# First attention's output product by pairs of feature tiles, most of it behind the units of the attention

## The chip, the cores and the metric

The kernel runs on one core of one Trainium2 chip. The metric is the device time of one execution in microseconds (us). TensorE (PE) multiplies, VectorE (DVE), ScalarE (ACT) and GpSimd (POOL) work on elements, SyncE (SP) issues the loads. Each engine takes its own instructions in their order; a wait at the head of an engine's queue holds all that stands behind it.

## What is computed

Two transformer-like blocks run after one another on 512 tokens of width 1024; the change lies in the second block's first attention, a windowed attention with 16 query heads of 64 features and 2 key heads, over the 512 tokens and 256 context tokens:

```python
def softmax_with_sink(s, sink):
    m = jnp.maximum(jnp.max(s, axis=-1, keepdims=True), sink)
    p = jnp.exp(s - m)
    return p / (jnp.sum(p, axis=-1, keepdims=True) + jnp.exp(sink - m))
...
def window_gqa(hx, hc, wq, wk, wv, wo, sink, cos, sin, need_ctx):
...
    out_x = jnp.moveaxis(ob, 0, 1).reshape(B, L, A_HEADS_2 * HEAD_DIM) @ wo
    out_c = None
    if need_ctx:
        qc = (hc @ wq).reshape(B, C, A_KV_HEADS, G, HEAD_DIM)
        s = jnp.einsum('bqhgd,bkhd->bhgqk', qc, kc).astype(jnp.float32) * scale
        p = softmax_with_sink(s, sink_f).astype(vc.dtype)
        out_c = jnp.einsum('bhgqk,bkhd->bqhgd', p, vc).reshape(B, C, A_HEADS_2 * HEAD_DIM) @ wo
    return out_x, out_c
...
        x = layer_norm(alpha * x + g1 * ax, ln1_g[i], ln1_b[i])
```

## The kernel before

All activations are kept with features on the partitions: `X` and `O` are 8 feature tiles of 128 features by 768 columns (512 tokens, then 256 context tokens; `X_CTX` names these two column ranges). Products in float32 are made from rounded halves: a weight `w` is split into `whi` and `wlo`, an activation into `Ahi` and `Alo`, and each product is three matmuls (`whi*Ahi`, `whi*Alo`, `wlo*Ahi`). Weights arrive in blocks of 128x2048 in a ring of three slots (`RING`); POOL splits each half block with two instructions (L460, L462).

The first attention is 96 **units** (`UNITS`): 4 groups of heads, in each 6 query tiles (first the two of the context, then the four of the tokens), in each 4 heads. A unit's scores have 256 keys (context), 512 or 640 keys (tokens), and one column more for the sink. So one group is 24 units: 8 of 257 columns, 4 of 513, 8 of 641, 4 of 513. The loops of all engines go by a **step** u:

- PE (L994): `window_scores` of unit u (L937 the sink, L943, L944 and L946 the keys, L953 the masks); then `window_turn` of unit u-3, which transposes its probabilities (L969, 2, 4 or 5 transposes); then in three steps of four a part of `window_values` for the four heads of an earlier tile (L983).
- DVE (L1893): the maximum of unit u (L1899); in 8 later steps and before the first ones `take_query`, the low half of a query (L1869); the reciprocal of unit u-1 (L1908); in every fourth step `take_values`, which moves values to `O` (L1853).
- ACT (L1399): `take_turned` of unit u-3, which copies the transposed probabilities to `ptA` (L1142), then the exponential of unit u (L1409), then in the steps of `TAKE_AT` (33, 35, 37, 39 and 63, 65, 67, 69 among others) the high half of a query (L1142).
- POOL (L556): scales the probabilities of unit u (L559) after its reciprocal.

The scores of unit u wait for the exponential of unit u-2, since two score buffers alternate. The turned probabilities have two PSUM buffers (banks 4 and 5 by turns; a fifth tile is put in bank 7), the values take bank 6.

After the last unit ACT and DVE split `O` tile by tile into `Ahi` and `Alo`, and `dense("woA", ...)` (L1008) multiplies it by the output weights, 8 output tiles by 8 input tiles, in all eight banks. DVE adds each output tile times `mod(0, 2, j, c)` to `X` (L1921), and the layer normalization `l1` begins with sums over all of `X` (L622). POOL splits block `B_WOA` ahead of the units, and the other blocks of this product after the last unit.

## Time and profile before

| what | us |
|---|---|
| median of 3 runs | 2848.58 |
| lowest, highest | 2844.63, 2852.0 |
| the profiled execution, its time | 2846.66 |
| its span | 2844.8 |
| PE busy in the span | 2670.7 (94%) |
| DVE, ACT, POOL busy | 1270.2, 663.3, 1332.8 |

Times in the trace are us from the span's start. A row of a timeline gives the start, the duration, the engine, the line and the tiles; x5 means five instructions merged. The busy time of a matmul includes its way through the array, so the distance from one start to the next is the better measure of its cost.

### The profile page before, as it was taken

Reading aid. Unit: us, or ns where it says so; the run is one execution under the profiler, and the core shown is the slowest. Engines: PE = TensorE matmul, PEld = TensorE weight load, DVE = VectorE, ACT = ScalarE, POOL = GpSimd, SP = SyncE. Lnnn points to the kernel's source line nnn. Section 1 sums busy time; section 2 is a strip of 40 time slices with the busy share of each in tenths; the row PEclk is TensorE's granted clock in tenths of the full one; section 3 lists DMA queues with packets and bytes.
Section 4 is the critical chain, followed back from the end, with each engine's and each line's share of the span. In section 5 each row is a group of like instructions: output and inputs, shape, how many; then the busy total and the mean of one; then the engine's idle time right before and its main releaser. Section 6 shows DMA issues by size and latency. Waiting matters only on the chain.

```text
span 2844.8 us, 39295 instructions
## 1 busy us (share of the span) xinstructions
PE 2670.7 (94%) x14668; PEld 2155.6 (76%) x14668; DVE 1270.2 (45%) x1904; ACT 663.3 (23%) x1255; POOL 1332.8 (47%) x862
## 2 busy tenths in 40 slices
PE   8989999999999989899989999999879998899997
PEld 6667777777777768666768888888668876778886
DVE  6941222252222245444354444444666554455545
ACT  2221000031000023566121110110345553211112
POOL 6356555535555553133546333444253221676661
PEclk9999999999999989899989999999999998999998
DMA  5124444434444431000111111111101100222221
GB/s 189 45 82 150 146 147 145 143 105 143 146 139 141 141 125 67 23 1 1 45 38 60 60 63 62 59 59 59 45 30 44 44 29 23 79 91 96 96 96 52
DMA packets 67369, 235.57 MB, mean 83 GB/s; under 512 B 8144, under 2 KB 9552, under 8 KB 67152
## 3 DMA queue, kind: packets, MB, share of 16 engines
q1 hardware_dynamic: 65792, 233.64, 25.0%
q8 instruction: 62, 1.02, 0.1%
q10 hardware_dynamic: 1488, 0.69, 0.1%
q14 instruction: 27, 0.22, 0.0%
HBM read 232.21 MB, written 2.10 MB: 82 GB/s over the span
## 4 chain that ended last, share of the span: by engine, by line
PE 86%; DVE 5%; issue 4%; ACT 2%; POOL 1%; DMA 1%; DVEq 0%; SPq 0%; ACTq 0%; POOLq 0%
PE ps L589 67%; PE ps L1084 2%; PE ps L780 2%; PE ps L744 2%; PE ps L983 2%; PE ps L1056 1%; PE ps L969 1%; PE ps L1106 1%; DMA raw<-in_stream 1%; DVE X L1953 1%; PE ps L708 1%; PE ps L632 1%; PE ps L937 1%; PE ps L944 1%; PE ps L789 1%
## 5 line engine op out<-in xcount | busy, mean ns | idle before, releaser
L460 POOL TENSOR_SCALAR whi<-raw 128x1024 fp32r<-128x1024 f32 x332 | 362.8, 1093 | 1189.3 <-DMA raw<-in_stream 1189.1
L462 POOL TENSOR_TENSOR wlo<-raw,whi 128x1024 fp32r<-128x1024 f32 x332 | 812.9, 2449 | 27.7
L589 PE MATMUL ps<-Ahi,whi 128*128 128x512 f32 (+1 forms) x2128 | 730.0, 374 | 37.1 <-DVE Alo L1573 17.8
L589 PE MATMUL ps<-Alo,whi 128*128 128x512 f32 (+1 forms) x2128 | 721.4, 370 | 0.0
L589 PE MATMUL ps<-Ahi,wlo 128*128 128x512 f32 (+1 forms) x2128 | 719.2, 369 | 0.0
L589 PEld LDWEIGHTS ps<-Ahi,whi 128*128 128x128 f32 x2128 | 375.9, 190 | 128.4 <-issue 21.9
L589 PEld LDWEIGHTS ps<-Ahi,wlo 128*128 128x128 f32 x2128 | 375.6, 190 | 69.5
L589 PEld LDWEIGHTS ps<-Alo,whi 128*128 128x128 f32 x2128 | 376.9, 191 | 66.9 <-issue 0.7
L589 PE MATMUL ps<-hhi,whi 128*128 128x512 f32 x1120 | 375.5, 372 | 19.5 <-DVE X L1953 18.8
L589 PE MATMUL ps<-hhi,wlo 128*128 128x512 f32 x1120 | 372.8, 370 | 0.0
L589 PE MATMUL ps<-hlo,whi 128*128 128x512 f32 x1120 | 370.2, 367 | 0.0
L1953 DVE SCALAR_TENSOR_TENSOR X<-ps,modT,X 128x512 f32<-128x512 f32 (+1 forms) x384 | 237.1, 654 | 91.5 <-PE ps L589 90.1
L1142 ACT ACTIVATE arena<-ps 128x256 f32<-128x256 f32 (+5 forms) x228 | 115.3, 519 | 629.7 <-PE ps L780 471.3
L1939 DVE TENSOR_TENSOR tmp<-tmp 128x768 f32<-128x768 f32 (+1 forms) x64 | 83.2, 1302 | 387.2 <-ACT tmp L1435 369.9
L1716 DVE TENSOR_TENSOR tmp<-ps,tmp 128x512 f32<-128x512 f32 x44 | 28.7, 687 | 490.8 <-PE ps L589 490.8
L589 PEld LDWEIGHTS ps<-hhi,whi 128*128 128x128 f32 x1120 | 192.5, 188 | 64.3 <-DVE X L1953 25.0
L589 PEld LDWEIGHTS ps<-hhi,wlo 128*128 128x128 f32 x1120 | 192.4, 188 | 39.3
L589 PEld LDWEIGHTS ps<-hlo,whi 128*128 128x128 f32 x1120 | 192.4, 188 | 38.1
L1435 ACT ACTIVATE tmp<-ps 128x512 f32<-128x512 f32 x96 | 47.1, 526 | 675.9 <-PE ps L589 673.7
L1729 DVE TENSOR_TENSOR X<-ps,X 128x512 f32<-128x512 f32 x176 | 121.4, 690 | 103.3 <-PE ps L589 100.9
L1142 ACT ACTIVATE hhi<-tmp 128x512 fp32r<-128x512 f32 (+1 forms) x108 | 74.8, 698 | 285.8 <-DVE tmp L1716 201.1
L559 POOL TENSOR_SCALAR tmp<-tmp,sm 128x256 f32<-128x256 f32 (+2 forms) x96 | 63.0, 658 | 158.8 <-DVE sm L1908 158.6
(267 smaller groups left out, 2842.2 us busy)
## 6 DMA issues: line engine op xcount, KB each, us to landing
raw<-in_stream SPq DMA_DIRECT2D x428, 512.0 KB, 3.7
X<-in_xT SPq DMA_DIRECT2D x2, 1024.0 KB, 6.5
arena<-in_dft SPq DMA_DIRECT2D x1, 2048.0 KB, 16.6
out_xT<-X SPq DMA_DIRECT2D x2, 1024.0 KB, 4.3
X<-in_ctxT SPq DMA_DIRECT2D x1, 1024.0 KB, 19.0
w<-in_stream SPq DMA_DIRECT2D x2, 512.0 KB, 4.3
vec<-in_vec SPq DMA_DIRECT2D x1, 364.5 KB, 7.6
arena<-in_fmap SPq DMA_DIRECT2D x1, 256.0 KB, 12.1
```

What stands on the lines that cost most here:

```text
L460: pool.tensor_scalar(whi[:, s, part], raw[:, s, part], 1.0, 1.0, ALU.mult, ALU.mult).then_inc(sem("w_hi"), 1)
L462: pool.tensor_tensor(wlo[:, s, part], raw[:, s, part], whi[:, s, part], ALU.subtract).then_inc(sem("w_split"), 1)
L559: pool.tensor_scalar(prob, prob, sm[:, u % 8, 2:3], 1.0, ALU.mult, ALU.mult).then_inc(sem("pA"), 1)
L589: mm = pe.matmul(dst[c], w[:, b % RING, off:off + P], rhs(k, part, c0, n), start=(k == 0 and w is whi and part == 0), stop=(k == kn - 1 an ...
L744: mm = pe.matmul(ps[:, WOUT_BANK[j], :], w[:, at:at + P], a[:, k, 0:T], start=(k == 0 and w is hi and a is Ahi), stop=(k == KT - 1 and w i ...
L780: mm = pe.matmul(ps[ADA_GROUP * g:ADA_GROUP * (g + 1), 6 + e, 0:256], csil[:, k, :], raw[:, at % RING, k * 256:(k + 1) * 256], start=(half ...
L983: mm = pe.matmul(ps[DH * h:DH * h + DH, 6, 0:2 * P], vA[:, ks[t], DH * g:DH * g + DH], heads[:, h], start=(t == 0), stop=(t == len(ks) - 1 ...
L1084: mm = pe.matmul(ps[:, 6 + t % 2, 0:256], a[:, k, t * P:(t + 1) * P], w[:, (B_QKV + 2) % RING, k * 256:(k + 1) * 256], start=(k == 0 and a ...
L1142: return act.activation(dst, src, ACT.Copy, scale=scale)
L1729: dve.tensor_tensor(X[:, m, 0:T], ps[:, 4 + m % 2, :], X[:, m, 0:T], ALU.add).then_inc(sem(f"{name}_dfree"), 1)
L1939: dve.tensor_tensor(tmp[:, j, 0:width], r, r, ALU.mult).then_inc(sem(f"{name}_mul"), 1)
L1953: mm = dve.scalar_tensor_tensor(out=X[:, m, c0:c0 + n], in0=ps[:, 4 + len(cols) * (m % (4 // len(cols))) + c, 0:n], scalar=mod(l, 5, m, c) ...
```

## The change

The product of the first attention is no longer made by output tiles over all of `O`. It is made by pairs of input tiles: pair p holds the feature tiles 2p and 2p+1 of `O`, which are complete once the 24 units of one group of heads are done. For each pair, each output tile m and each of the two column ranges c there is one **piece**: 6 matmuls of 512 or of 256 columns, and one DVE instruction that adds the result to `X`. There are 64 pieces. Of the 48 pieces of pairs 0 to 2, 46 stand at the end of PE's steps 33, 35, 36, 38, 39, ... 101 (`FILLED`), two in every three steps, even pieces 512 wide and odd ones 256 wide; they all use bank 7. The last two and the 16 of pair 3 follow after the loop, those of pair 3 in all banks. A piece waits until DVE has added the piece before it.

DVE adds the piece of PE's step u in its own step u+1, behind the maximum, `take_query`, the reciprocal and `take_values`. ACT and DVE split a pair's two tiles inside the loop (`pair_hi` in steps 32, 56, 80; `pair_lo` in steps 33, 57, 81); the weights of pairs 1 to 3 are split by POOL between the units (`pair_weights`, three smaller instructions a half block), and SP loads them with other rows and columns per block. The turned probabilities have one buffer (bank 4, a fifth tile in bank 5), and the transposes wait until the previous unit's are copied. `modulations(1)`, small DVE work, is moved ahead to the projection of the queries.

```diff
--- before.py
+++ after.py
+PIECES = [(p, m, c) for p in range(4) for m in range(KT) for c in range(2)]
+FILL_FIRST = 33
+FILLED = {FILL_FIRST + 3 * (i // 2) + 2 * (i % 2): i for i in range(48)}
+PAIR_HI = {24 * p + 32: p for p in range(3)}
+PAIR_LO = {24 * p + 33: p for p in range(3)}
+PAIR_SPLITS = {1: (4, 6, 8, 10, 12, 14), 2: (18, 20, 22, 24, 26, 28), 3: (66, 68, 70, 72, 74, 76)}
 V_FIRST = 2
...
+        def pair_split(p, kk):
+            return (Alo[:, 6 + kk, :], kd_r[:, kk, :]) if p % 2 else (Alo[:, 2 + kk, :], Alo[:, 4 + kk, :])
+        def piece_bank(i):
+            p, m, c = PIECES[i]
+            return 7 if p < 3 else 2 * (m % 4) + c
+        def piece_done(i):
+            p, m, c = PIECES[i]
+            if m % 4 == 3 and c:
+                return when("w_used", 2 * (B_WOA + p) + m // 4 + 1)
+            return when("woA_done", i + 1 - i // 8)
         def v(name, i, n=1):
             a = _cols[name][0] + i
...
             split_swiglu(1)
-            split_run(B_KV, ring_end(B_WOA))
+            split_run(B_KV, B_WOA + 1)
+            def pair_weights(p, step):
+                b, half, step = B_WOA + p, step // 3, step % 3
+                if step == 0:
+                    part = slice(half * HALF, (half + 1) * HALF)
+                    pool.wait_ge(*when(f"raw{b % RING}{half}", 16 * (b // RING) + 16))
+                    pool.tensor_scalar(whi[:, b % RING, part], raw[:, b % RING, part], 1.0, 1.0, ALU.mult,
+                                       ALU.mult).then_inc(sem("w_hi"), 1)
+                    return
+                part = slice(half * HALF + (step - 1) * 512, half * HALF + step * 512)
+                pool.wait_ge(*when("w_hi", SPLITS[b] + half + 1))
+                mm = pool.tensor_tensor(wlo[:, b % RING, part], raw[:, b % RING, part], whi[:, b % RING, part], ALU.subtract)
+                if step == 2:
+                    mm.then_inc(sem("w_split"), 1)
             for u in range(N_UNITS):
+                for p, units in PAIR_SPLITS.items():
+                    if u in units:
+                        pair_weights(p, units.index(u))
                 pool.wait_ge(*when("denA", u + 1))
                 prob = probA[u % 4][:, 1:1 + len(keys(UNITS[u][2])) * P]
...
                                        ALU.add).then_inc(sem(f"{name}_res"), 1)
-            split_run(ring_end(B_WOA), ring_end(B_ML0 + 2))
+            split_run(B_ML0, ring_end(B_ML0 + 2))
             norm_residual("l1", 1, X_CTX)
             split_run(ring_end(B_ML0 + 2), ring_end(B_QKV + 2))
...
             def turned(u, t):
-                at = (4 + u % 2) * 512 + t * P if t < 4 else 7 * 512
+                at = 4 * 512 + t * P if t < 4 else 5 * 512
                 return psf[:, at:at + P]
             def window_turn(u):
                 ks = keys(UNITS[u][2])
                 pe.wait_ge(*when("pA", u + 1))
-                pe.wait_ge(*when("ptA", u + 1))
+                pe.wait_ge(*when("ptA", u + 2))
                 for t in range(len(ks)):
-                    if t == 4:
-                        pe.wait_ge(*when("ptA", u + 2))
                     mm = pe.transpose(turned(u, t), probA[u % 4][:, 1 + t * P:1 + (t + 1) * P], ident[:, :])
                 mm.then_inc(sem("turnA"), 1)
...
+            def out_piece(i):
+                p, m, c = PIECES[i]
+                b, (c0, n) = B_WOA + p, X_CTX[c]
+                if m % 4 == 0 and c == 0:
+                    pe.wait_ge(*when("w_split", SPLITS[b] + m // 4 + 1))
+                if m == 0 and c == 0:
+                    pe.wait_ge(*when("OA_split", 2 * p + 2))
+                before = i if p < 3 or i < 56 else i - 7
+                if i > 0:
+                    pe.wait_ge(*when("woA_evac", min(before, 48) if p == 3 and i < 56 else before))
+                for kk in range(2):
+                    hi, lo = pair_split(p, kk)
+                    at = m // 2 * 512 + kk * 256 + m % 2 * P
+                    for w, o in ((whi, hi), (whi, lo), (wlo, hi)):
+                        mm = pe.matmul(ps[:, piece_bank(i), 0:n], w[:, b % RING, at:at + P], o[:, c0:c0 + n],
+                                       start=(kk == 0 and w is whi and o is hi), stop=(kk == 1 and w is wlo))
+                mm.then_inc(sem("w_used" if m % 4 == 3 and c else "woA_done"), 1)
             pe.wait_ge(*when("maskb", 2))
                 four, part = divmod(u - LEAD - 4, 4)
                 if four >= 0 and part < 3:
                     window_values(four, part)
-            dense("woA", B_WOA, X_CTX, "OA_split")
-            pe.wait_ge(*when("woA_evac", 5))
-            layernorm("l1", X_CTX, "woA_evac", 0)
+                if u in FILLED:
+                    out_piece(FILLED[u])
+            for i in range(max(FILLED[u] for u in FILLED if u < N_UNITS + LEAD + 3) + 1, len(PIECES)):
+                out_piece(i)
+            pe.wait_ge(*when("woA_evac", 48 + 10))
+            layernorm("l1", X_CTX, "woA_evac", 48, 2)
...
-                four = (4 + u % 2) * 512
+                four = 4 * 512
                 act.wait_ge(*when("turnA", u + 5))
                 act.wait_ge(*when("oA_done", u // 4 + 1))
                 if nk > 4:
-                    copy(ptA[u // 4 % 2][:, 4, h * P:(h + 1) * P], psf[:, 7 * 512:7 * 512 + P])
+                    copy(ptA[u // 4 % 2][:, 4, h * P:(h + 1) * P], psf[:, 5 * 512:5 * 512 + P])
                     nk = 4
                 copy(ptA[u // 4 % 2][:, 0:nk, h * P:(h + 1) * P],
                      psf[:, four:four + nk * P].rearrange("p (t q) -> p t q", t=nk)).then_inc(sem("ptA"), 1)
+            def pair_hi(p):
+                act.wait_ge(*when("oA", 6 * p + 7))
+                if p >= 2:
+                    act.wait_ge(*block_used(B_WOA + p - 2))
+                for kk in range(2):
+                    copy(pair_split(p, kk)[0], O[:, 2 * p + kk, :]).then_inc(sem("OA_hi"), 1)
             for u in range(N_UNITS + LEAD):
                 if u >= LEAD:
                         take_query(*TAKE_AT[u])
                     if u == KEYS_AT:
                         take_keys(1)
-            for k in range(KT):
-                if k == 0:
-                    act.wait_ge(*when("oA", 25))
-                copy(Ahi[:, k, :], O[:, k, :]).then_inc(sem("OA_hi"), 1)
+                if u in PAIR_HI:
+                    pair_hi(PAIR_HI[u])
+            pair_hi(3)
             layernorm("l1", X_CTX, 1)
...
                     take_keys(0)
                     for h in range(2):
                         take_query(0, 0, h)
+                if j == 4:
+                    modulations(1)
             for h in (2, 3):
                 take_query(0, 0, h)
             dve.wait_ge(*when("vA", 1))
                 dve.wait_ge(*when("oA_done", four + 3))
                 move(O[:, 4 * g + 2 * e:4 * g + 2 * e + 2, n * P:(n + 1) * P],
                      ps[:, 6, 0:2 * P].rearrange("p (a q) -> p a q", a=2)).then_inc(sem("oA"), 1)
+            def pair_lo(p):
+                for kk in range(2):
+                    dve.wait_ge(*when("OA_hi", 2 * p + kk + 1))
+                    hi, lo = pair_split(p, kk)
+                    dve.tensor_tensor(lo, O[:, 2 * p + kk, :], hi, ALU.subtract).then_inc(sem("OA_split"), 1)
+            def add_piece(i):
+                p, m, c = PIECES[i]
+                c0, n = X_CTX[c]
+                if i == 0:
+                    dve.wait_ge(*when("n5_res", KT))
+                dve.wait_ge(*piece_done(i))
+                dve.scalar_tensor_tensor(out=X[:, m, c0:c0 + n], in0=ps[:, piece_bank(i), 0:n], scalar=mod(0, 2, m, c),
+                                         in1=X[:, m, c0:c0 + n], op0=ALU.mult, op1=ALU.add).then_inc(sem("woA_evac"), 1)
             for u in range(N_UNITS + LEAD + 4):
                 if u < N_UNITS:
                 four, part = divmod(u - LEAD - 7, 4)
                 if four >= 0 and part == 0:
                     take_values(four)
-            for k in range(KT):
-                split_lo("OA_split", "OA_hi", k, O[:, k, :], TT)
-            dve.wait_ge(*when("n5_res", KT))
-            for j in range(8):
-                if j % 2:
-                    dve.wait_ge(*block_used(B_WOA + j // 2))
-                else:
-                    dve.wait_ge(*when("woA_done", j // 2 + 1))
-                for c, (c0, n) in enumerate(X_CTX):
-                    mm = dve.scalar_tensor_tensor(out=X[:, j, c0:c0 + n], in0=ps[:, 2 * (j % 4) + c, 0:n],
-                                                  scalar=mod(0, 2, j, c), in1=X[:, j, c0:c0 + n], op0=ALU.mult, op1=ALU.add)
-                mm.then_inc(sem("woA_evac"), 1)
-                if j == 3:
-                    modulations(1)
+                if u in PAIR_LO:
+                    pair_lo(PAIR_LO[u])
+                if u - 1 in FILLED and u - 1 < N_UNITS + LEAD + 3:
+                    add_piece(FILLED[u - 1])
+            pair_lo(3)
+            for i in range(FILLED[max(u for u in FILLED if u < N_UNITS + LEAD + 3)] + 1, len(PIECES)):
+                add_piece(i)
             layernorm("l1", X_CTX, 1)
```

In step 36 PE has, before (line numbers of before), the scores of unit 36, the transposes of unit 33, and then the next scores; `waits` lists the semaphores:

```order
L937 MATMUL ps<-vec,ident 128x1 [waits sA_free]
L944 MATMUL ps<-std_r,Ahi 128x256
L946 MATMUL ps<-std_r,Ahi 128x384
L953 MATMUL ps<-maskb 128x128 x2
L944 MATMUL ps<-rstd_r,Ahi 128x256
L946 MATMUL ps<-rstd_r,Ahi 128x384
L969 MATMUL ps<-ident,tmp 128x128 [waits ptA,pA]
L969 MATMUL ps<-ident,tmp 128x128 x3
L937 MATMUL ps<-vec,ident 128x1 [waits sA_free]
```

The same step of PE in the changed kernel, from the last matmul of the piece of step 35 (L1066 is a piece, L1000 the sink, L1030 a transpose):

```order
L1066 MATMUL ps<-Alo,wlo 128x256
L1000 MATMUL ps<-vec,ident 128x1 [waits sA_free]
L1007 MATMUL ps<-std_r,Ahi 128x256
L1009 MATMUL ps<-std_r,Ahi 128x384
L1016 MATMUL ps<-maskb 128x128 x2
L1007 MATMUL ps<-rstd_r,Ahi 128x256
L1009 MATMUL ps<-rstd_r,Ahi 128x384
L1030 MATMUL ps<-ident,tmp 128x128 [waits ptA,pA]
L1030 MATMUL ps<-ident,tmp 128x128 x3
L1066 MATMUL ps<-Alo,whi 128x512 [waits woA_evac]
```

A piece stands in front of the scores and one behind the transposes, and the second waits for DVE. On DVE the steps 33 to 35 were:

```order
L1899 TENSOR_REDUCE sm<-ps 128x1 [waits sA]
L1869 TENSOR_TENSOR q_63<-arena,q_63 64x768 [waits qs_hi]
L1908 RECIPROCAL sm<-sm 128x1 [waits sA_free]
L1899 TENSOR_REDUCE sm<-ps 128x1 [waits sA]
L1908 RECIPROCAL sm<-sm 128x1 [waits sA_free]
L1853 TENSOR_SCALAR arena<-ps 128x2x128 [waits oA_done]
L1899 TENSOR_REDUCE sm<-ps 128x1 [waits sA]
```

In the changed kernel, up to the add of the piece of step 35 in step 36:

```order
L2005 TENSOR_REDUCE sm<-ps 128x1 [waits sA]
L1958 TENSOR_TENSOR q_64<-arena,q_64 64x768 [waits qs_hi]
L2014 RECIPROCAL sm<-sm 128x1 [waits sA_free]
L1988 TENSOR_TENSOR Alo<-arena,Alo 128x768 [waits OA_hi] x2
L2005 TENSOR_REDUCE sm<-ps 128x1 [waits sA]
L2014 RECIPROCAL sm<-sm 128x1 [waits sA_free]
L1942 TENSOR_SCALAR arena<-ps 128x2x128 [waits oA_done]
L1996 SCALAR_TENSOR_TENSOR X<-ps,modT,X 128x512 [waits woA_done,res]
L2005 TENSOR_REDUCE sm<-ps 128x1 [waits sA]
L1958 TENSOR_TENSOR q_64<-arena,q_64 64x768 [waits qs_hi]
L2014 RECIPROCAL sm<-sm 128x1 [waits sA_free]
L2005 TENSOR_REDUCE sm<-ps 128x1 [waits sA]
```

The pair's low halves stand behind a `take_query`, and each add behind the maximum and the reciprocal of its step.

## Rows read from the trace of the kernel before

**Rows 1.** Window, steps 33 on: PE, PEld, DVE, ACT, POOL busy, clock, DMA, GB/s.

```profile
1232.00:1360.20 128.20, 119.17 (x869) 84.39 (x867) 59.44 (x152) 86.49 (x223) 47.97 (x68) 1.00 0.00 1
```

**Rows 2.** Timeline of the last values (PE), and the chain of waits behind it.

```profile
1358.19 1.95 PE L983 MATMUL ps<-ptA,arena 128*64 128x256 f32 x16 [0.69 <-ACT ptA L1142]
```
```profile
1363.24 69.57 PE ps L589 x384
```

**Rows 3.** Timeline, PE: one step of 641 columns with values.

```profile
1252.60 0.38 PE L937 MATMUL ps<-vec,ident 128*128 128x1 f32 x2
1253.70 0.71 PE L969 MATMUL ps<-ident,tmp 128*128 128x128 f32 x5
1254.34 1.08 PE L983 MATMUL ps<-ptA,arena 128*64 128x256 f32 x8
```

**Rows 4.** Timelines, PE: ten matmuls of 512 columns, and six of 256, apart.

```profile
2600.01 0.40 PE L589 MATMUL ps<-hhi,wlo 128*128 128x512 f32 x1
...
2602.35 0.39 PE L589 MATMUL ps<-hhi,whi 128*128 128x512 f32 x1
```
```profile
2090.41 0.28 PE L1084 MATMUL ps<-wlo,Ahi 128*128 128x256 f32 x1
...
2091.12 0.28 PE L1084 MATMUL ps<-wlo,Ahi 128*128 128x256 f32 x1
```

**Rows 5.** Waits of PE between 1232 and 1361: us, times, longest.

```profile
PE ps L969 <- POOL tmp L559: 6.7, 5, 1.7
```

**Rows 6.** Groups by form, DVE: busy and mean ns, then idle time before them.

```profile
L1899 DVE TENSOR_REDUCE sm<-ps 128x1 f32<-128x641 f32 x24 | 19.7, 820 | 14.6 <-PE ps L946 14.6
L1853 DVE TENSOR_SCALAR arena<-ps 128x256 f32<-128x256 f32 x17 | 6.9, 406 | 2.3 <-PE ps L983 2.3
L1899 DVE TENSOR_REDUCE sm<-ps 128x1 f32<-128x257 f32 x16 | 6.8, 425 | 14.7 <-PE ps L944 14.6
```
```profile
L1921 DVE SCALAR_TENSOR_TENSOR X<-ps,modT,X 128x512 f32<-128x512 f32 x8 | 6.0, 746 | 45.5 <-PE ps L589 45.5
L1921 DVE SCALAR_TENSOR_TENSOR X<-ps,modT,X 128x256 f32<-128x256 f32 x8 | 3.8, 474 | 0.0
```

**Rows 7.** Timeline of step 63, with a query taken: PE, ACT, DVE.

```profile
1288.07 0.71 PE L969 MATMUL ps<-ident,tmp 128*128 128x128 f32 x5
...
1289.47 0.80 ACT L1409 ACTIVATE tmp<-ps,sm 128x641 f32<-128x641 f32 x1
...
1291.11 0.95 DVE L1869 TENSOR_TENSOR Ahi<-arena,Ahi 64x768 fp32r<-64x768 f32 x1 [2.01 <-ACT Ahi L1142]
...
1292.17 0.81 DVE L1899 TENSOR_REDUCE sm<-ps 128x1 f32<-128x641 f32 x1
...
1292.89 0.15 DVE L1908 RECIPROCAL sm<-sm 128x1 f32<-128x1 f32 x1
```

**Rows 8.** Timeline of steps 32 and 33: transposes, maximum, next ACT copy.

```profile
1229.45 0.38 PE L969 MATMUL ps<-ident,tmp 128*128 128x128 f32 x2
...
1229.65 0.69 DVE L1899 TENSOR_REDUCE sm<-ps 128x1 f32<-128x513 f32 x1 [1.75 <-PE ps L943]
...
1230.48 0.38 PE L969 MATMUL ps<-ident,tmp 128*128 128x128 f32 x2
...
1231.06 0.37 ACT L1142 ACTIVATE ptA<-ps 128x256 f32<-128x256 f32 x1
```

**Rows 9.** Timeline after the last unit: splits of `O` beside POOL's splits of weights.

```profile
1360.64 4.51 ACT L1142 ACTIVATE Ahi<-arena 128x768 fp32r<-128x768 f32 x6 [2.51 <-DVE arena L1853]
1361.52 6.45 DVE L1542 TENSOR_TENSOR Alo<-arena,Ahi 128x768 fp32r<-128x768 f32 x3 [0.91 <-ACT Ahi L1142]
```

**Rows 10.** Page, costliest groups: POOL's low half of a weight block.

```profile
L462 POOL TENSOR_TENSOR wlo<-raw,whi 128x1024 fp32r<-128x1024 f32 x332 | 812.9, 2449 | 27.7
```

**Rows 11.** Windows of PE alone: length, busy, granted clock, DMA.

```profile
1203.00:1206.00 3.00, 3.00 (x13) 0.50 0.02 5
...
1363.30:1366.60 3.30, 3.30 (x11) 0.51 0.00 0
```

29 lines of the change are left out of this document (23 added, 6 removed).

## The prediction, made before the changed kernel was run

> **What bounds the kernel now.** I read the page first (PE busy 94%, and the chain that ended last is 86% PE), then the windows around the first attention, then PE's timeline step by step, since PE's order is what the change rewrites. Two stretches matter: the units from step 33 on, and the output product behind them. In the units PE is busy for 119.17 of 128.20 us [rows 1], so 9.0 us are idle as the profile counts it; 6.7 us of them are five waits for POOL's scaled probabilities [rows 5], which come late in the steps where a query is taken. Some more is hidden in matmul durations that include the way through the array: 0.1 to 0.2 us in about thirty steps. I take 14.5 us as the most that other work could fill there. Behind the units, the values end at 1358.19 + 1.95 = 1360.14, the product starts at 1363.24 and takes 69.57 us without a break [rows 2], up to 1432.81: 72.7 us from the last value to the end of the product. So TensorE sets the pace in both stretches. Moving multiplications from the second into the first gives nothing by itself; it can give the 14.5 us of idle time, and it costs whatever new waits PE meets.
>
> **The pieces themselves: no work saved.** 512-column matmuls follow at (2602.35 - 2600.01)/10 = 0.234 us, 256-column ones at (2091.12 - 2090.41)/6 = 0.118 us [rows 4]. A piece of six costs 1.40 or 0.71 us, a pair of pieces 2.11 us, and the 32 such pairs 67.6 us; the old product, 192 times one of each, took 69.57. Of the pieces 23 even and 22 odd ones (47.9 us) come before the last values, the rest after.
>
> **The end of the attention.** Let t be the end of the last values, on the old clock 1360.14. Piece 45 runs to t+0.7, its add to t+1.2. Piece 46 (waiting for that add) runs to t+2.7. The halves of the last two tiles of `O`: ACT starts at t+0.5 [rows 9], a copy takes 0.83, DVE's low half 0.95 if undisturbed [rows 7], but 6.45/3 = 2.15 while POOL splits weights beside it [rows 9], which it will do here as before, with blocks of the next layer. The first low half ended at about 1363.2 before, so both are done at about t+4.0. Then come the add of piece 46 (0.75), piece 47, its add, and piece 48 at t+6.0; sixteen pieces more take 16.9 us: t+22.9. Together 47.9 + 22.9 = 70.8 against 72.7: **-1.9 us**. Half a lost stretch of clock (below) is as likely here as before, so I take **-1**; from -3 to +2.
>
> **New wait 1: one bank, and the add behind the next maximum.** Even pieces from step 36 on follow an odd piece of the step before. The even piece waits for the odd one's add, which DVE has behind the maximum of this step. Count from the first transpose of the step. The maximum starts 0.20 us later [rows 8], occupies DVE for 0.72 (from 1292.17 to 1292.89 [rows 7]), the reciprocal about 0.07, the add 0.474 [rows 6], a semaphore 0.06: 1.53 us, and 1.86 in steps with `take_values` (0.406 [rows 6], 0.33 of it not overlapped). For units of 257 columns the maximum is 0.40 shorter [rows 6]. PE meanwhile has the transposes (0.64 for five up to the values, 0.54 up to a piece, 0.43 for four, 0.21 for two) and in some steps 1.0 us of values [rows 3]. With values of that length the add is hidden. Without: step 42 1.3, 54 1.3, 60 1.1, 78 1.3, 84 1.1, 90 1.3, and 45 and 93 0.2 each: **7.8 us**. Odd pieces have a whole step for the add before them and wait only where a query is taken.
>
> **New wait 2: adds behind a taken query.** In steps 33, 35, 37, 39 and 63, 65, 67, 69 DVE's `take_query` stands between the maximum and the rest, and waits for exponential and copy on ACT. In step 63 it ran from 1291.11 to 1292.06, that is 3.99 us after the transposes at 1288.07 [rows 7]. Then reciprocal and add follow: 4.0 + 0.1 + 0.47 + 0.06 = 4.6 us (4.9 with a 512-wide add of 0.746). In steps 39 and 63 PE has 1.65 us to do: 2.95 us of waiting each. In step 69 it has 1.2: 3.2. The piece of step 38 waits for an add of step 37: 4.9 less the 2.1 us of steps 37 and 38 up to the piece, 2.8; that of step 68 for one of 67, where values cover most, 0.5. In steps 36 and 66 the maximum itself starts late, behind the query of the step before: 1.3 and 2.2. Together **15.9 us**. None of these adds exists before, so the price is built from DVE's own order; its lower bound is 5 us, if ACT reaches the copies sooner because PE is slower, the upper 18.
>
> **New wait 3: the first piece of a pair.** Its operands are split inside the loop. For pairs 1 and 2: in step 56 ACT is free for `pair_hi` 1.6 us after the transposes (1229.45 to 1231.06 in step 32, which has the same shape [rows 8]); one copy 0.83, then two low halves of 0.95 each (the second copy runs beside the first of them), 2.75 us with the semaphore, so PE may start the piece at 4.4 us; it is there at 1.03 (1230.48 - 1229.45 [rows 8]) + 0.21: 3.15 us of waiting, twice. For pair 0 the high halves (1.7 us) push back the exponential of unit 33, behind that are copy (0.8) and low half (0.95) of a query, and only then the two low halves of the pair: exponential of 33 starts at 1231.06 + 1.7 + 0.37 = 1233.1, ends at 1233.8, copy to 1234.6, query to 1235.55, low halves to 1237.5; PE would be there at 1230.8: **6.8 us**. The sum is **13.1 us**, from 8 to 15. The Trainium skill (SBUF — State Buffer, "SBUF: two separate sides") says that a DVE instruction with two SBUF inputs and a GpSimd instruction take the shared port pair as an exclusive lock. The 2.15 us of [rows 9] against 0.95 of [rows 7] agree with it; by it POOL's scaling, released 0.2 us before, would slip between the two low halves and add up to 0.8 us a pair, 2.4 in all, to the sum. I leave that to the range.
>
> **What the waits give back.** A step in which PE waits for an add is one in which exponentials and POOL catch up, so most of the 14.5 us of old idle time goes. Taken at **-12.5** (-9 to -14.5).
>
> **Clock.** PE ran at its upper level throughout the units after 1232 although it waited up to 1.7 us five times [rows 1, 5]. But in 1203 to 1206 the granted clock was 0.50, and in 1363.3 to 1366.6 it was 0.51 right after PE had stood still for 3.1 us [rows 11, 2]: 1.2 instead of 2.4 GHz, a loss of 1.7 us each time. The new waits of over 2 us are eight (steps 33, 38, 39, 57, 63, 66, 69, 81). I take two or three such falls, **+4** (0 to +12).
>
> **The rest.** One turned buffer: the copy of unit u-4 follows the exponential of unit u-2, for which the scores of step u wait anyway; the copy (0.37 to 0.77) is shorter than those scores (0.56 to 1.10 [rows 3]). Nothing, at most 2 us over the many short steps. POOL's 18 smaller splits (12 of them half of 2.449, 1.2 us [rows 10]) stand before a scaling of 0.5 to 0.8, whose result is wanted three steps later: covered; at most 3 us in the short steps 4 to 28. `modulations(1)` is small work in the queries' projection, where DVE has three instructions for each output tile and waits for PE, as it was beside PE's product before: nothing. Loads of the next weights wait for later pieces, but POOL has two blocks ready and the normalization to split the third in. Together **+0.5**.
>
> **The sum.** 7.8 + 15.9 + 13.1 = 36.8 us of new waits, -12.5, -1, +4, +0.5: **+27.8 us**. On the profiled execution's own 2846.66 this is 2874.5; the median of the runs shown is 1.9 higher, 2848.58, which gives 2876.4. I say 2875.
>
> **Rivals.**
> (a) The pieces fill the idle time and hardly wait: DVE is idle for over half of the stretch (59.44 of 128.20 [rows 1]) and each add is only 0.5 to 0.75 us, so the adds would be there in time. This decides the sign if waits 1 to 3 stay under 10 us together. Then -12.5 - 1 + 5 = -8.5 us or more, down to -16: about 2836. Against it: DVE is idle because it waits for scores, and the adds stand behind those waits in its queue.
> (b) Waits and gains cancel: ACT and DVE run ahead because PE has 1.05 us more per step, wait 2 falls to 5 us, wait 3 to 8, wait 1 to 4: 17 - 12.5 - 1 + 1.5 = +5: about 2853.
> (c) The clock falls at nearly each long wait, and the port lock adds its share: +27.8 + 8 + 3 = 2887 and more.
> The Trainium skill (Perfetto Trace Analysis, "Matmuls") says that independent matmul groups should rotate through PSUM banks, so that the eviction of one overlaps the next group. It speaks against bank 7 for all 46 pieces. By it, two banks for the pieces would take away wait 1 (7.8 us) and most of wait 2; the changed kernel has one left, the others hold scores, turned probabilities and values.
>
> **Chances.** The forecast with (c): 0.84, slower by over 0.3%, which is 8.5 us and about what a measurement of this kernel can tell from no change. (b) 0.10, within 0.3%. (a) 0.06, faster. The range 2854 to 2890 leaves out (a), half of (b) and the far end of (c).
>
> **What would show it.** In the changed kernel PE's waits should name DVE's add (`X`) before pieces, some 20 times, about 24 us; DVE's low halves before the first piece of pairs 0, 1, 2 with about 7, 3 and 3 us; the stretch from step 33 to the last values should grow from 128 us by 48 + 24 + 4 to about 202 us; from the last values to the end of the product about 23 us instead of 72.7. The waits for POOL in steps 35 to 39 and 63 to 69 should be gone. If the stretch is at 170 us or less, the waits were overestimated; if waits for POOL grow in steps 4 to 28, the weight splits were not covered.

## The result and the profile after

The changed kernel took **2888.66 us** (median of 4 runs, 2887.13 to 2890.40), the kernel before 2848.84 us (median of 4, 2844.63 to 2852.00). The ratio is 1.0138, with a 95% interval of 1.0117 to 1.0159: 39.8 us slower, where 26.4 (2875 against 2848.58) were forecast. The profiled execution took 2888.75 us, with a span of 2887.0 (before 2844.8) and a mean granted clock of 0.963 (before 0.974).

To see where the 42.2 us of the spans lie I cut both traces at three marks on PE: the first sink matmul of unit 0, that of step 33, that of step 95, and the first sum of the normalization behind the output product. The windows show us, then the busy time of PE, PEld, DVE, ACT and POOL with counts of instructions, the granted clock, DMA share and GB/s. Before:

```profile
1166.30:1229.60 63.30, 57.14 (x369) 41.94 (x370) 29.45 (x76) 42.09 (x109) 19.08 (x31) 0.87 0.00 1
1229.67:1351.71 122.04, 113.41 (x824) 81.31 (x823) 58.71 (x148) 84.12 (x217) 41.83 (x62) 1.00 0.01 1
1351.71:1432.74 81.03, 77.24 (x443) 64.47 (x441) 28.19 (x46) 10.36 (x18) 42.23 (x25) 0.98 0.14 46
```

The same stretches of the changed kernel:

```profile
1163.20:1228.70 65.50, 58.54 (x370) 42.59 (x371) 29.53 (x77) 42.28 (x109) 32.78 (x43) 0.86 0.00 1
1228.70:1438.50 209.80, 176.27 (x1070) 132.94 (x1070) 84.63 (x194) 88.77 (x223) 53.13 (x68) 0.88 0.04 13
1438.50:1474.00 35.50, 33.08 (x197) 25.36 (x195) 17.97 (x33) 6.08 (x12) 19.17 (x13) 1.00 0.09 30
```

The chain of waits from the last values on (start, us, what), which answers to [rows 2]:

```profile
1451.41 0.92 PE ps L1066 x6
...
1452.84 1.80 DVE kd_r L1988 x2
1454.64 0.71 DVE X L1996
...
1457.05 17.03 PE ps L1066 x96
```

The three stretches together grew from 266.4 to 310.8 us, 44.4 more; the rest of the program gave 2 back. The tail fell by 45.5 us, the stretch of the units grew by 87.8, and the first 33 steps by 2.2. The 246 more matmuls of the middle stretch are the 41 pieces 0 to 40, 43.6 us of work at the upper clock level. So 44 us of the 87.8 are something else, and the clock column names one part of it: 0.88 where it was 1.00.

PE's waits of the changed kernel from 1228 to 1457 (releaser: us in total, times, longest), which answer to the five waits for POOL of [rows 5]. Of those for adds, 27.9 us in 17 times stand between the units and 1.4 us in two times behind the last:

```profile
PE ps L1066 <- DVE X L1996: 29.3, 19, 3.5
PE ps L1066 <- DVE Alo L1988: 5.3, 1, 5.3
```

Behind step 33 POOL is gone as a releaser, and the adds (`X`) and the low halves (`Alo`) have come. The long wait is the first piece of pair 0. Timeline of step 33 (start, duration, engine, line, operation; in brackets the idle time before it and who ended it):

```profile
1229.91 1.56 ACT L1225 ACTIVATE Alo<-arena 128x768 fp32r<-128x768 f32 x2
...
1231.64 0.69 ACT L1499 ACTIVATE tmp<-ps,sm 128x513 f32<-128x513 f32 x1
...
1233.17 0.95 DVE L1958 TENSOR_TENSOR q<-arena,q 64x768 fp32r<-64x768 f32 x1 [2.02 <-ACT q L1225]
...
1234.23 1.81 DVE L1988 TENSOR_TENSOR Alo<-arena,Alo 128x768 fp32r<-128x768 f32 x2
1234.41 2.11 POOL L622 TENSOR_SCALAR tmp<-tmp,sm 128x512 f32<-128x512 f32 x1 [4.57 <-DVE sm L2014]
```

High halves, exponential, query, low halves: the order that the prediction followed, 1.4 us shorter than it made it. An add behind a taken query, in step 38:

```profile
1252.48 0.60 PE L1030 MATMUL ps<-ident,tmp 128*128 128x128 f32 x4
...
1253.81 0.95 DVE L1958 TENSOR_TENSOR q<-arena,q 64x768 fp32r<-64x768 f32 x1 [1.74 <-ACT q L1225]
...
1254.87 0.73 DVE L1996 SCALAR_TENSOR_TENSOR X<-ps,modT,X 128x512 f32<-128x512 f32 x1
...
1255.66 0.80 PE L1066 MATMUL ps<-Alo,whi 128*128 128x256 f32 x2 [2.57 <-DVE X L1996]
```

DVE waits 1.74 us for ACT's copy of the query, and PE waits for the add behind it. All waits read in this way, step by step:

| step | 33 | 36 | 38 | 39 | 42 | 45 | 54 | 57 | 60 |
|---|---|---|---|---|---|---|---|---|---|
| predicted, us | 6.8 | 1.3 | 2.8 | 2.95 | 1.3 | 0.2 | 1.3 | 3.15 | 1.1 |
| measured, us | 5.35 | 0.93 | 2.57 | 2.15 | 1.15 | 0.20 | 1.08 | 2.85 | 0.93 |

| step | 63 | 66 | 68 | 69 | 78 | 81 | 84 | 90 | 93 |
|---|---|---|---|---|---|---|---|---|---|
| predicted, us | 2.95 | 2.2 | 0.5 | 3.2 | 1.3 | 3.15 | 1.1 | 1.3 | 0.2 |
| measured, us | 2.89 | 2.93 | 0.55 | 3.46 | 1.08 | 2.85 | 0.93 | 1.15 | 0.20 |

That is 33.3 us against 36.8. The waits were nearly what was forecast; the missing time of this execution is the clock. These are the stretches of PE at the lower level (us, PE busy, granted clock, DMA, GB/s); in the kernel before, none lies between 1206 and 1361:

```profile
1224.80:1245.20 20.40, 15.05 (x52) 0.50 0.00 0
1255.50:1262.20 6.70, 6.46 (x27) 0.50 0.00 0
1265.70:1269.00 3.30, 3.30 (x17) 0.50 0.00 0
1317.00:1323.60 6.60, 6.60 (x27) 0.50 0.01 2
1337.40:1344.00 6.60, 6.06 (x21) 0.50 0.00 1
1351.10:1357.70 6.60, 5.79 (x21) 0.50 0.00 0
1368.10:1371.40 3.30, 3.10 (x9) 0.50 0.00 0
```

At 0.50 (1.2 instead of 2.4 GHz) a piece of 512 columns shows its price in the chain of waits (start, us, what), beside one at the upper level:

```profile
1368.30 2.90 PE ps L1066 x6
...
1378.15 1.59 PE ps L1066 x6
```

In the seven stretches PE is busy for 46.4 us. At the upper level that work takes half, so the lower clock costs at most 23 us. Behind step 33 the stretches last 50.6 us from end to end (the windows above are set a little inside) with PE busy for 43, so I put the cost there at some 21. The balance of the middle stretch is then 43.6 (pieces) + 33.3 (waits) + 21 (clock) = 98, less 87.8 measured: 10 us of old idle time came back. Of these, 8.4 can be named: the waits that PE had before and has no more, 6.7 us for POOL and 1.7 us for ACT's exponentials.

### The profile page after: what moved, and what is told of

It reads as the page before. It is cut to its first block, busy times and chain, and to the rows that moved or that the text cites. A ratio compares the mean times of both kernels' runs of the same rounds, so it can differ in the third digit from the quotient of the medians.

```text
span 2887.0 us, 39293 instructions
## 1 busy us (share of the span) xinstructions
PE 2687.7 (93%) x14668; PEld 2167.1 (75%) x14668; DVE 1284.3 (44%) x1952; ACT 663.8 (23%) x1255; POOL 1335.6 (46%) x868
## 4 chain that ended last, share of the span: by engine, by line
PE 83%; DVE 8%; issue 4%; ACT 2%; POOL 2%; DMA 1%; DVEq 0%; SPq 0%; ACTq 0%; POOLq 0%
PE ps L652 61%; PE ps L1066 3%; PE ps L1167 2%; PE ps L843 2%; PE ps L807 2%; PE ps L1139 1%; PE ps L1044 1%; PE ps L1030 1%; PE ps L1189 1%; POOL X L629 1%; DVE X L2052 1%; PE ps L771 1%; PE ps L1007 1%; PE ps L695 1%; DVE X L1673 1%
## 5 line engine op out<-in xcount | busy, mean ns | idle before, releaser
L504 POOL TENSOR_SCALAR whi<-raw 128x1024 fp32r<-128x1024 f32 x326 | 355.8, 1091 | 1164.3 <-DMA raw<-in_stream 1163.9
L506 POOL TENSOR_TENSOR wlo<-raw,whi 128x1024 fp32r<-128x1024 f32 x326 | 797.3, 2446 | 27.2
L652 PE MATMUL ps<-Ahi,whi 128*128 128x512 f32 x2000 | 694.4, 375 | 33.5 <-DVE Alo L1662 17.6
L652 PE MATMUL ps<-Alo,whi 128*128 128x512 f32 x2000 | 686.3, 371 | 0.0
L652 PE MATMUL ps<-Ahi,wlo 128*128 128x512 f32 x2000 | 684.9, 370 | 0.0
L652 PEld LDWEIGHTS ps<-Ahi,whi 128*128 128x128 f32 x2000 | 355.3, 190 | 121.5 <-issue 23.6
L652 PEld LDWEIGHTS ps<-Ahi,wlo 128*128 128x128 f32 x2000 | 355.2, 190 | 65.5
L652 PEld LDWEIGHTS ps<-Alo,whi 128*128 128x128 f32 x2000 | 355.9, 190 | 63.2 <-issue 0.7
```

Of the source, the lines that this page charges most:

```text
L504: pool.tensor_scalar(whi[:, s, part], raw[:, s, part], 1.0, 1.0, ALU.mult, ALU.mult).then_inc(sem("w_hi"), 1)
L506: pool.tensor_tensor(wlo[:, s, part], raw[:, s, part], whi[:, s, part], ALU.subtract).then_inc(sem("w_split"), 1)
L652: mm = pe.matmul(dst[c], w[:, b % RING, off:off + P], rhs(k, part, c0, n), start=(k == 0 and w is whi and part == 0), stop=(k == kn - 1 an ...
```

## The experiments

"The three stretches" below is the time from the first sink of unit 0 to the normalization: 266.4 us before, 310.8 after. Their parts, always in this order, are steps 0 to 32, steps 33 to 94, and the tail. Each kernel computes everything.

**The changed kernel again**, with no edit.

> The changed kernel itself once more, so that it stands on the same chip as the next three, and for the spread of its times, since a second trace shows what of the half-clock stretches repeats. Both theories: 1.2 to 1.6% over before. If the clock's falls come from the long waits, the second trace has them at the same waits (half clock for 25 to 55 us between step 33 and the end of the units).

It took 2891.07 us (2887.82 to 2897.08, 4 runs), 1.0136 of before [1.0117, 1.0155]. The three stretches are 310.6 us, with 50.4 us at the lower clock behind step 33 (50.6 the first time), in seven pieces that start 4.4 us later than in the first trace and are as long, behind the same waits. So the falls are no accident of one execution. But the two traced executions are not typical in their clock: the mean granted clock over the whole kernel is 0.963 in both, and 0.966 to 0.969 in the six others of this kernel, which took 2887.1 to 2891.5 us; 0.001 of the mean is 5.8 us at the lower level, which is half. The kernel before had 0.974 where it was traced and 0.965 to 0.973 in its 78 executions beside the experiments. How long the lower level held behind step 33 in the executions without a trace is not known, and may be less than 50 us.

**The add at the head of DVE's step.** The add now comes before the maximum and the query of the next step, which takes the queue away and leaves the one bank:

```
             for u in range(N_UNITS + LEAD + 4):
+                if u - 1 in FILLED and u - 1 < N_UNITS + LEAD + 3:
+                    add_piece(FILLED[u - 1])
                 if u < N_UNITS:
...
                 if u in PAIR_LO:
                     pair_lo(PAIR_LO[u])
-                if u - 1 in FILLED and u - 1 < N_UNITS + LEAD + 3:
-                    add_piece(FILLED[u - 1])
```

> The changed kernel with one thing moved: DVE adds the piece of the step before at the front of its step, ahead of the maximum, instead of at its end. Bank, number of pieces and PE's order are the same. Theory A (the waits for the adds come from their place in DVE's queue): of the 29.3 us that PE waited for adds (L1996) between step 33 and the end of the units, all but 2 to 5 us go (left at steps 36 and 66, where DVE is still late from a taken query, and at the end), and with the 2 to 3 us waits some of the half-clock time; the whole is 25 to 35 us faster than the changed kernel's 2888.7, about 2857. Theory B (one bank is the cause, whatever the place of the add): PE goes on waiting 15 us or more for the adds, and the time stays over 2875. Theory C (it is POOL's splits and the pair starts that cost): no more than 5 us faster.

It took 2867.0 us (2861.89 to 2874.13, 10 runs), 1.0052 [1.0036, 1.0069]: more than half of the loss is gone. PE's waits between 1200 and 1457:

```profile
PE ps L1030 <- POOL tmp L622: 6.1, 6, 1.7
PE ps L1066 <- DVE Alo L1988: 5.4, 1, 5.4
PE ps L1066 <- DVE X L1996: 5.1, 4, 2.1
PE ps L1066 <- issue: 4.8, 2, 2.4
```

```profile
1233.20:1412.70 179.50, 165.95 (x1070) 126.64 (x1069) 88.01 (x195) 89.06 (x223) 53.10 (x68) 0.92 0.05 16
```

The waits for adds fell from 29.3 to 5.1 us, and between the units from 27.9 to 1.8 (step 66); 4.8 us more, at the starts of pairs 1 and 2, now have no releaser named. Of the waits for POOL, 5.0 us stand ahead of step 33, as long as in the changed kernel, and of the five of [rows 5] only one of 1.1 us is back. The middle stretch fell by 30.3 us, of which about 10 are clock: 29.9 us at the lower level instead of 50.6. What made the pieces wait was the place of the add in DVE's order. The rule that the prediction quoted from the Trainium skill (Perfetto Trace Analysis, "Matmuls": rotate PSUM banks) speaks to these waits too, but with one bank and the add in front 24 of the 29 us went. No kernel here has a second bank between the units, so what it would bring there is not shown.

**The pieces three steps later, so that none waits for the splits of its pair.**

```
-FILL_FIRST = 33
+FILL_FIRST = 36
```

> The changed kernel with the first piece in step 36 instead of 33 (so the pairs begin in steps 36, 60, 84, three steps behind the splitting of their tiles, and 44 pieces instead of 46 stand inside the loop). Theory A: the three waits for the low halves at the pair starts (5.3 us in step 33, 2.85 in each of 57 and 81) go, 11 us; two pieces more stand behind the units, each waiting for its add, +1.5 us; the clock, which fell before step 33, may stay up sooner, 0 to 8 us. Together 8 to 17 us faster than 2888.7, about 2876. Rival: pair 0's splitting delays the exponential of unit 33 anyway, and the wait only moves to the transposes of steps 34 to 36: then 5 us or less.

2890.35 us (2881.71 to 2891.98, 4 runs), 1.0131 [1.0094, 1.0169]: no gain in the median. In its trace only the long wait of step 33 is gone. Steps 57 and 81 wait 2.76 us each instead of 2.85, since DVE still has the two low halves ahead of the add, and the transposes of step 35 wait 2.2 us for POOL where they had no wait: in part the rival's case. The three stretches are 301.1 us there, 9.7 fewer, but that execution was the fastest of the four; the other three lie at 2889.1 to 2892.0. A gain of a few us can't be told from these.

**The weight splits of pair 2 in steps 42 to 54 instead of 18 to 28.**

```
-PAIR_SPLITS = {1: (4, 6, 8, 10, 12, 14), 2: (18, 20, 22, 24, 26, 28), 3: (66, 68, 70, 72, 74, 76)}
+PAIR_SPLITS = {1: (4, 6, 8, 10, 12, 14), 2: (42, 44, 46, 50, 52, 54), 3: (66, 68, 70, 72, 74, 76)}
```

> The changed kernel with POOL's six instructions for the weights of pair 2 in steps 42 to 54 instead of 18 to 28, where PE does not yet have pieces. Steps 27 to 33 took 3.1 us more in the changed kernel than before, with new waits for POOL's scaled probabilities (0.3, 0.9 and 0.6 us), and the granted clock was at half from the end of that stretch on for 20 us. Theory A: those 3.1 us go, nothing comes instead, since the steps 42 to 54 are long; without a fall of the clock in front of step 33 another 2 to 6 us go; in all 3 to 9 us. Theory B (splits are covered everywhere, the clock falls for other reasons): less than 1.5 us.

2890.39 us (2884.64 to 2898.82, 4 runs), 1.0139 [1.0100, 1.0179]: again none in the median, and again the profiled execution was the fastest. Its trace still answers the question on POOL. In the changed kernel PE waits for POOL's scalings in steps 27 (0.3 us), 30 and 31:

```profile
1222.52 1.27 POOL L612 TENSOR_TENSOR wlo<-raw,whi 128x512 fp32r<-128x512 f32 x1
1222.61 0.44 PE L1030 MATMUL ps<-ident,tmp 128*128 128x128 f32 x2 [0.94 <-POOL tmp L622]
...
1224.30 0.44 PE L1030 MATMUL ps<-ident,tmp 128*128 128x128 f32 x2 [0.62 <-POOL tmp L622]
```

The kernel before has the wait of step 30 too:

```profile
1226.29 0.44 PE L969 MATMUL ps<-ident,tmp 128*128 128x128 f32 x2 [0.95 <-POOL tmp L559]
```

It is there without the splits as well (0.95 us), and so is that of step 27 (0.32), which the kernel with one buffer of turned probabilities also has. Only the wait of step 31 goes with the splits: its scaling stands behind the split at 1222.52. Steps 27 to 32 took 9.5 us before, 12.6 in the changed kernel and 10.0 in this one.

In the changed kernel the clock fell right behind step 31 (1224.7) and stayed down until after the long wait of step 33. Without those splits it stayed up until that long wait was under way (times of the kernel with later splits: us, PE busy, clock):

```profile
1224.00:1234.00 10.00, 6.54 (x46) 1.00 0.01 2
1234.00:1240.80 6.80, 2.84 (x8) 0.50 0.00 0
```

Steps 0 to 32 take 64.3 us instead of 65.5, and behind step 33 30.7 us are at the lower level. But the long wait of step 33 is 6.5 us instead of 5.35: what PE gains ahead of it, it waits for ACT and DVE there.

**One buffer of turned probabilities, in the kernel before.**

```
-                at = (4 + u % 2) * 512 + t * P if t < 4 else 7 * 512
+                at = 4 * 512 + t * P if t < 4 else 5 * 512
...
-                pe.wait_ge(*when("ptA", u + 1))
+                pe.wait_ge(*when("ptA", u + 2))
```

> The kernel before with one part of the change alone: one buffer of turned probabilities (bank 4, a fifth tile in bank 5), and the transposes of a unit wait until the unit before is copied. Theory A: the copy is done by the time the scores in front of the transposes are; 0 to 2 us slower than before's 2848.8. Rival: the missing second buffer is a good part of the 40 us: 5 us or more slower, with new waits of PE's transposes for ACT's copies.

2855.03 us (2849.98 to 2864.26, 10 runs), 1.0011 [0.9994, 1.0029]; three stretches of 267.0 us. It costs nothing that can be measured, as predicted. Its trace has one stretch of 3.4 us at the lower level, right behind a wait of 1.6 us for POOL in step 35; the kernel before has that wait (1.6 us) and stayed at the upper level.

**All three edits together** (add first, pieces from 36 on, splits of pair 2 later).

> The changed kernel with all three edits of the first runs: adds at the front of DVE's step, first piece in step 36, POOL's splits for pair 2 in steps 42 to 54. With the adds in front alone, the stretch from the first unit to the normalization was 281.6 us (before 266.4, changed kernel 310.8); still in it were 10 us of waits at the three pair starts, 5 us for adds, 6 us for POOL, and 30 us at half clock. Theory A (these are separate causes that add up): 10 us of waits, 2 to 3 us of POOL and half of 15 to 25 us of half clock less, 1.5 us more behind the units: about 258 to 264 us, so 3 to 8 us faster than before. Theory B (PE has no idle time worth filling): over 270 us, slower than before by 4 us or more.

2856.92 us (2851.28 to 2862.69, 10 runs), 1.0020 [1.0008, 1.0033]. The three stretches are 274.0 us, not the 258 to 264 expected: the middle is 166.4, but the tail is 44.6, since now the clock is at its lower level there, and pieces stand behind short waits for adds. By its numbers this is the outcome of theory B; the last kernels below, with shorter tails, speak against its reason in their traces. Its chain of waits:

```profile
1410.32 0.99 PE ps L1066 x6
...
1411.87 2.71 PE ps L1066 x6
...
1415.41 1.66 PE ps L1066 x6
```

**The waits alone.** The kernel before, with its own product behind the units, and nothing but eight waits of PE for the taken query at the end of steps 33, 35, 37, 39, 63, 65, 67 and 69. This separates "waits cost their own length" from "waits bring the clock down":

```
                 if four >= 0 and part < 3:
                     window_values(four, part)
+                if u in TAKE_AT and u >= 33:
+                    g, e, h = TAKE_AT[u]
+                    pe.wait_ge(*when("qs", 8 * g + 4 * e + h + 1))
```

> The kernel before, with nothing but PE made to wait: at the end of steps 33, 35, 37, 39, 63, 65, 67 and 69 it waits for the query that DVE finishes in that step, 2.3 to 3.4 us each, some 22 us, of which 6 to 8 us replace old waits for POOL in the steps behind. No pieces, no splits, no second use of banks. Theory A (long waits of PE pull the clock down): besides the 14 to 16 us of waiting, a granted clock of 0.5 for 10 to 25 us between steps 33 and 72, another 5 to 12 us; 20 to 27 us slower than before. Theory B (the clock falls in the changed kernel because of something in the pieces, not the waits): the clock stays at 1.00, 14 to 16 us slower.

2870.45 us (2868.56 to 2876.37, 4 runs), 1.0075 [1.0054, 1.0096]. Waits of PE between 1229 and 1450, the window of the units, and PE's windows at the lower level:

```profile
PE ps L937 <- DVE Ahi L1872: 10.9, 4, 3.5
PE ps L937 <- DVE q L1872: 10.0, 4, 3.2
```

```profile
1228.20:1375.60 147.40, 125.03 (x824) 89.87 (x823) 59.96 (x148) 84.04 (x217) 41.94 (x62) 0.88 0.00 1
```

```profile
1232.20:1238.80 6.60, 6.35 (x24) 0.50 0.00 0
1242.40:1252.50 10.10, 6.93 (x31) 0.50 0.01 2
1303.90:1317.30 13.40, 9.92 (x43) 0.50 0.00 1
1331.20:1334.40 3.20, 3.20 (x15) 0.50 0.00 0
```

The 824 matmuls are the same as before, and the clock column still reads 0.88. The stretch grew by 25.4 us: 20.9 of new waits, less the 6.7 of [rows 5] that they cover, plus half of the 26.4 us in which PE is busy at the lower level, gives 27.4. Eight waits of 1.3 to 3.5 us are enough to bring the clock down for 34 us; neither the pieces nor their shape is needed. By the prediction's own size, two or three falls of 1.7 us, the stretch would have grown by 18. All this is the traced execution. In the medians the kernel lost 19.1 us, of which the net waits are 14.2, so some 5 are left for the clock: the trace shows the falls, and the medians a smaller price than the 13 us of its balance.

**Halves of a pair apart.** The kernel with all three edits, and in it `pair_hi` and `pair_lo` each split over two steps (24p+32 and +34, 24p+34 and +36) and the pieces from step 39 on.

```
-FILL_FIRST = 36
+FILL_FIRST = 39
...
-PAIR_HI = {24 * p + 32: p for p in range(3)}
-PAIR_LO = {24 * p + 33: p for p in range(3)}
+PAIR_HI = {24 * p + 32 + 2 * kk: (p, kk) for p in range(3) for kk in range(2)}
+PAIR_LO = {24 * p + 34 + 2 * kk: (p, kk) for p in range(3) for kk in range(2)}
```

> As the kernel with all three edits, but the two copies of a pair on ACT two steps apart (steps 32 and 34 and so on) and so the low halves (34 and 36), with the first piece in step 39. No step then has both a taken query and two copies and two low halves. Theory A: the waits for POOL behind steps 33 to 37 shrink by 2 to 4 us, the third of a fall of the clock there; 0 to 6 us faster than the kernel with the three edits, and with it faster than before by 5 to 12 us. Rival: two fewer pieces in the loop leave idle time unfilled and the tail longer, 0 to 3 us slower than it.

2858.7 us (2848.86 to 2869.52, 10 runs), 1.0028 [1.0010, 1.0045]: not faster than all three together. The middle fell by 5.9 us to 160.5, with only 6.8 us at the lower level; the tail rose by 4.0 to 48.6, because two pieces more (six instead of four) wait for each other's adds there, and the last low halves took 2.8 us instead of 1.8, beside a split of POOL.

**The tail's pieces in free banks.** Added to the kernel with the halves apart: behind the last unit banks 0 to 5 are free, so its pieces 42 to 47 take them without waiting. This is the bank rule, applied where nothing else is left to cover an add.

```
-            return 7 if p < 3 else 2 * (m % 4) + c
+            return i - LOOPED if LOOPED <= i < 48 else 7 if p < 3 else 2 * (m % 4) + c
...
-                if i > 0:
+                if i > 0 and not LOOPED <= i < 48:
```

> The kernel with all three edits and the halves apart, with one edit more: the six pieces of pair 2 that stand behind the units take banks 0 to 5, which are free by then, and do not wait for the add before them. Theory A (one bank costs most where there are no units between the pieces): the tail behind unit 95 was 48.6 us with 6.8 us at half clock; six waits of 0.5 to 1 us go, and with the shorter gap in part the fall of the clock: 4 to 7 us less, so the stretch from the first unit to the normalization is 266 to 269 us, equal to before's 266.4, the time within 0.1% of before. Rival (the gap at the end is the splitting of the last pair, whatever the banks): under 2 us.

2849.31 us (2841.61 to 2856.83, 12 runs), 0.9990 [0.9976, 1.0004]. The tail fell from 48.6 to 38.7 us, and the lower clock in it is gone. (In its trace the first 33 steps took 67.9 us, with 25.9 at the lower clock, ahead of anything that the edit touches; the sum of the three stretches, 267.1, holds 4 us of that.) What is left of the gap is DVE's, in the chain of waits (low halves, then six adds):

```profile
1413.50 2.84 DVE kd_r L1989 x2
1416.34 3.16 DVE X L1997 x6
...
1419.64 17.03 PE ps L1067 x96
```

**All 64 pieces behind the units**, over eight banks: the low and high halves of pairs 0 and 1 are made between the units, but no piece is. It asks whether it pays to run pieces between the units at all. The part of the edit in PE's loop (the banks, the waits for adds, and the places of the splits are changed to fit):

```
-                if u in FILLED:
-                    out_piece(FILLED[u])
-            for i in range(max(FILLED[u] for u in FILLED if u < N_UNITS + LEAD + 3) + 1, len(PIECES)):
+            for i in range(len(PIECES)):
                 out_piece(i)
```

> The product in pairs and pieces as in the changed kernel, but no piece among the units: all 64 stand behind them, over all eight banks, a piece waiting for the add of the eighth before it. The tiles of pairs 0 and 1 are split among the units (two steps apart), those of pairs 2 and 3 behind them. One buffer of turned probabilities, as in the changed kernel. Theory A (the loss comes from pieces among the units, pieces as such cost nothing; a pair's operands are ready when the units end): the 64 pieces take 67.6 us, the start gap of 2.8 us and the fall of the clock behind it (1.7 us) go, some waits for POOL behind the copies in steps 32 to 36 come: 0 to 5 us faster than before (stretch 262 to 266 us). Rival (small pieces cost in themselves, 64 adds instead of 16, weights in another order): the tail is longer than before's 81.0 us, and the time 3 us or more over before.

2854.09 us (2847.36 to 2860.93, 12 runs), 1.0006 [0.9994, 1.0019]. The chain of waits:

```profile
1363.65 1.95 PE ps L1046 x16
1365.59 67.39 PE ps L1069 x384
```

The product follows the last values without the 3.1 us gap of [rows 2], and the tail is 76.3 us instead of 81.0. But steps 33 to 94, with no piece in them, lost 7.3 us: PE waits for POOL 8.3 us in 7 times there instead of 6.7 in 5, since POOL splits the weights of two pairs between its scalings (low halves of 1.28 us each), and 6.8 us are at the lower clock. These two make some 5 us of the 7.3; the rest I haven't found.

**The last pair sooner.** Added to the one with the tail's free banks: the low halves of pair 3 stand between the adds of the tail's pieces instead of ahead of them, and the pieces of pair 3 wait for the add of their own bank only.

```
-            pair_lo(3)
-            for i in range(FILLED[max(u for u in FILLED if u < N_UNITS + LEAD + 3)] + 1, len(PIECES)):
+            for i in range(LOOPED, len(PIECES)):
                 add_piece(i)
+                if i == LOOPED + 1:
+                    pair_lo(3)
```

> The kernel with the tail banks, with the end of the units mended once more: DVE splits the low halves of the last pair after the adds of two of the six tail pieces instead of before all six, and the first pieces of pair 3 wait only for the add whose bank they take. In the kernel with the tail banks PE stood still for about 3.4 us in front of pair 3 (the last tail piece done at 1416, pair 3 begun at 1419.6, with the six adds behind the low halves). Theory A: the six pieces cover the splitting, 2 to 3.5 us less behind unit 95 (38.7 to about 35.5 us), the time 2846 to 2849 on the chip of the runs, 0.1 to 0.25% under before. Rival: the low halves are held up by POOL's splits of the next weights and the gap stays: under 1 us.

2845.91 us (2841.72 to 2852.47, 12 runs) against 2849.14 (17 runs): 0.9987 [0.9974, 1.0000]. Chain of waits:

```profile
1400.01 1.01 PE ps L1045 x8
1401.02 24.01 PE ps L1069 x138
```

From the last values to the normalization PE never stops. The three stretches are 260.5 us against 266.4 in the two traces; the medians differ by 3.2. This is the fastest kernel of the study, 0.13% under the one before, and its interval touches 1; at this size it isn't shown to be faster.

## Why the prediction was right and where it was not

The direction and the mechanism were right, the size was short by 13 us. The median lies 1.3 us inside the upper end of the range (2890), and that of the repeat, 2891.07, 1.1 us outside it, so that the range held is in part luck. The stretch from step 33 to the last values was to grow from 128 us by 76, which makes 204 and not the 202 written there; it grew by 92.2, from 130.5 to 222.7 us. From the 27.8 us forecast to the 42.2 of the traced spans: waits -3.5, what they give back +2.5, clock +17, pieces and tail -1, the rest -0.5. Step by step:

- **What bounds the kernel.** Right: both stretches are PE's, and pieces moved from one to the other brought no gain of their own (43.6 us in the units, 45.5 us less in the tail).
- **The end of the attention.** From the last values (to 1451.4) to the end of the product (1474.1) it took 22.7 us; 23 were forecast. Both low halves were done at t+3.2 instead of t+4.0, since they took 0.90 us each (POOL's split of weights was over 0.16 us after they began), and the last run of pieces started at t+5.6 instead of t+6.0.
- **Waits 1 and 2** were 7.8 and 15.9 us; their steps show 6.7 and 15.5. **Wait 3** was 13.1 and is 11.05: step 33 took 5.35 instead of 6.8. ACT had begun the high halves 0.3 us before the transposes, where I had put them 0.6 behind. The releaser is the add from step 36 on, also at steps 57 and 81, where I had named the low halves; the length (2.85 each) is theirs and the add's together, since DVE has both in a row, and the first experiment leaves 2.4 of it.
- **The port.** I had read the lock of the Trainium skill (SBUF — State Buffer, "SBUF: two separate sides") as putting POOL's scaling between the two low halves, at up to 0.8 us a pair. At each of the three pair starts the two low halves ran undisturbed (1.81 us), and POOL's scaling, which began 0.18 us behind the first of them, took 2.11 us, where the same form takes 0.69 elsewhere. So it did not slip between the two: it ended 0.5 us behind the second. The trace agrees with a lock, but the one held up was POOL, and nobody waits for that scaling there. Where POOL was first, DVE paid: with the halves apart, low halves that began 0.13 to 0.15 us behind a scaling took 1.35 us instead of 0.94, and one beside a split of weights 1.94.
- **What the waits give back** was 12.5 us; the balance above leaves about 10, if the clock cost 21.
- **Clock: the step that failed.** "I take two or three such falls, +4". Seven falls were there in both traces, up to 20.4 us long, and cost some 20 us in the units. The mechanism was named, but I had priced a fall by the two of [rows 11], 3.3 us at 0.50 each, single falls in a full or an ended stretch, and taken each wait by itself. Where waits of 1 to 3 us follow one another, the clock comes back late or falls again; the kernel with the waits alone shows this without any piece, and the repeated trace shows it in the same places. Rival (c), 2887 and more, was nearest in its sum, if for +8 of clock where it was about +20, and for a port that cost nothing.
- **The rest, POOL's splits: wrong too, but small.** "Covered; at most 3 us". The scaling behind the split of step 28 made PE wait 0.6 us, steps 27 to 32 took 3.1 us more, of which 2.6 went with the splits, and the clock fell there first. The prediction had said where this would be seen. One turned buffer was rightly put at nothing.
- **Rivals (a) and (b)** needed waits of under 10, or of 17 us; 33 were there.

What stays open: how much of the 20 us of clock each wait brings, and how much of it the executions without a trace had, whose mean clock was higher at nearly the same time. The second and third experiments took away the long wait of step 33 and the early splits one at a time; both traces have 30 us at the lower level behind step 33 instead of 50.6, but the medians of the two kernels moved by less than their spread, and only on top of the edit to the adds did the two count (1.0052 to 1.0020). Each of the two has one trace, of its fastest execution, so these can't be taken for their medians.

Of the loss of 1.38%, the place of DVE's adds is 0.86% (1.0138 to 1.0052, 24 us), the pair starts and the early splits together 0.32% (to 1.0020, 9 us). The free banks in the tail gave 0.38% more (1.0028 to 0.9990, 11 us), but to a kernel with six pieces waiting there; the changed kernel has two, so this is no share of its loss. In each of these three steps the two intervals do not touch. The gap ahead of the last pair (0.9990 to 0.9987) is within the spread.
